# The first attention's heads between parts of the cross values' weight slots, with a third of the convolution's taps in its steps

## The chip, the cores and the metric

The kernel runs on one core of one Trainium2 chip. The metric is the device time of one execution in microseconds (us). Before the change three runs took 1483.89, 1485.74 and 1492.4 us, so the median is 1485.74 us.

## What is computed

Two blocks in a row over 256 tokens of width 1024, all in float32. Only the first block's mixer and the key and value projections of its cross attention matter here:

```python
y = rmsnorm(h, norm_mix_g[l]) @ w_in[l]
q = partial_rotary(y[..., 0:D_ATT].reshape(B, S, ATT_HEADS, HEAD_DIM))
k = partial_rotary(y[..., D_ATT:2 * D_ATT].reshape(B, S, ATT_HEADS, HEAD_DIM))
v = y[..., 2 * D_ATT:3 * D_ATT].reshape(B, S, ATT_HEADS, HEAD_DIM)
att = dilated_sliding_attention(q, k, v).reshape(B, S, D_ATT)      # 8 heads of 64
conv = conformer_conv(...)        # a * sigmoid(g), depthwise convolution of 31 taps, layernorm, silu
h = h + jnp.concatenate([att, conv], axis=-1) @ w_out[l]
xq = (rmsnorm(h, norm_x_g[l]) @ w_xq[l])
mn = rmsnorm(mem, norm_mem_g[l])
xk = (mn @ w_xk[l])               # cross keys, from the memory alone
xv = (mn @ w_xv[l])               # cross values, from the memory alone
```

After it come the cross attention, a multilayer perceptron and the second block's two layers, the last one with eight experts. None of that is touched.

## The kernel before, in words

Every engine's program is written out by hand in its own function (`pe` for TensorE, `act` for ScalarE, `dve` for VectorE, `pool` for GpSimd, `sp` for SyncE), and engines meet at semaphores: `mark` counts an event, `after(...)` gives the count to wait for. Each engine carries out its own program strictly in the written order.

**Weights** come in slots of 1 MB. A ring of three raw slots (`weights`) is filled by SyncE. ScalarE's `high(n)` (line 1395) writes the rounded high part of a slot in two halves, and VectorE's `low(n)` (line 1869) writes what is left, in two halves too; the pair is `weights_split`, which has room for two slots. So `high` of slot j waits until TensorE has used slot j-2, and each half of `low` waits for the same half of `high`. TensorE takes three matmuls per product (`matmul3`, lines 532 to 534): high by high, high by low, low by high. A slot costs it 48 matmuls of 256 columns (`features_out`) or 24 of 512 columns, 12 for each of the two token tiles (`tokens_out`). Slots 10 to 13 are the cross keys (`xk`), 14 to 17 the cross values (`xv`), 18 to 21 the output projection (`wout`).

**Order on TensorE** before the change: slots of `g`, `a`, `q`, `k`, then the memory's turned rows, `v`, four slots of `xk`, four slots of `xv`, then 16 transposes of queries and keys (line 704, `qkT`), and then `attention`. Results go to a ring of four banks (`open_bank`); a bank is reused once ScalarE or VectorE has read it.

**The attention** is pipelined over steps s. In step s TensorE does `scores` of head s (line 713, two matmuls from 64 rows), the four transposes of head s-1's probabilities (line 646) and `outs` of head s-2 (line 666, into 64 columns). ScalarE does the two exponentials of head s (line 1452) and copies head s-1's turned probabilities (line 1467). VectorE first divides head s-1's probabilities by their sums (lines 1983 and 1987), then reads head s's scores and takes the negated maximum (lines 2001 and 2009), and in odd steps from 5 on splits a finished pair of heads (lines 1874 and 1876). All three functions have a hook `between(s)` that is called at the end of each step; the first attention leaves it empty.

**The convolution** is VectorE's: `conv_taps(n)` does n taps of a pair of channel tiles (line 2050, two instructions each), 62 taps in all, spread between the slots' `low`. After the attention comes the convolution's mean over channels: TensorE's `cmean` (line 723) waits for the last tap, VectorE subtracts it (line 2102), ScalarE squares, TensorE sums again (`cvar`), and after the scaling, the silu and a split TensorE can use the convolution's half of the features. Meanwhile TensorE does the attention's half of the output projection.

Of the kernel before, what the change touches and what calls it, by code (L numbers as in the profile page):

```python
# [11 lines left out]
P = 128  # L12
S = 256
TT = S // P
# [123 lines left out]
def program(nc, A, out, points, stop):  # L138
    ctx = ExitStack()
    with ctx:  # L140
# [231 lines left out]
        def after(*name):  # L372

            key, n = points.get(name, ("pe", 1))
            return sems[key], n
# [139 lines left out]
        with nc.Block() as block:  # L515
# [3 lines left out]
            def _(pe):  # L519
# [25 lines left out]
                def tokens_out(stage, actT, n, i=0, tag=(), midway=lambda: None):  # L545

                    ps = []
                    for r in range(2):
                        if r == 1:
                            midway()  # L550
                        j, w = weights(stage)
                        for t in range(TT):
                            if r == 0:
                                ps.append(open_bank(stage, *tag, i, t))
                            for k in range(4):
                                mm = matmul3(ps[t][:, 0:n], lambda z: actT[:, z, 4 * r + k, t * P:(t + 1) * P],
                                             lambda z: w[:, z, k, :], r == 0 and k == 0, r == 1 and k == 3)
                            if r == 1:
                                mm.then_inc(*cpe.mark("filled", stage, *tag, i, t))
                            elif t == 1:  # L560
                                mm.then_inc(*cpe.mark("slot", j))
                    cpe.also("slot", j)
# [93 lines left out]
                def pair_outs(stage, tag, v, until_now=False):  # L656

                    def outs(h, pt, u):
                        if h % 2 == 0:
                            ps = open_bank(stage, *tag, h // 2)  # L660
                        else:
                            ps = bank_of[(stage, *tag, h // 2)]
                        o = 64 * (h % 2)
                        for kt in range(TT):
                            first = kt * P if until_now else 0
                            mm = pe.matmul(ps[o:o + HD, first:S], v[:, kt, h * HD:(h + 1) * HD],  # L666
                                           flat(pt)[:, kt * S:(kt + 1) * S - first],
                                           start=(kt == 0), stop=(kt == TT - 1))
                        mm.then_inc(*cpe.mark("o", u))
                        if h % 2:  # L670
                            cpe.also("filled", stage, *tag, h // 2)
                    return outs
# [19 lines left out]
                turn_norm(1)  # L692
                tokens_out("v", HT, 512)
                pe.wait_ge(*after("ht", 1))
                for i in range(4):
                    features_out("xk", MT, "xk", i)
                for i in range(2):
                    tokens_out("xv", MT, 512, i)
                pe.wait_ge(*after("rotated"))
                for b in range(4):  # L700
                    ps = open_bank("qkT", b)
                    for c in range(2):
                        for t in range(TT):
                            mm = pe.transpose(ps[:, c * S + t * P:c * S + (t + 1) * P],
                                              QK[:, t, (2 * b + c) * P:(2 * b + c + 1) * P], ident)
                    mm.then_inc(*cpe.mark("filled", "qkT", b))
                pe.wait_ge(*after("read", "qkT", 3))
                pe.wait_ge(*after("read", "v", 0, 1))

                def scores1(h, ps):  # L710
                    o = 64 * (h % 2)
# [2 lines left out]
                                       QKT[o:o + HD, 4 + h // 2, :], start=True, stop=True)  # L714
                    return mm

                attention(0, AH, scores1, pair_outs("att_o", (), V))

                def mean_over_channels(name, need, src):
                    pe.wait_ge(*after(need))  # L720
# [631 lines left out]
            def _(act):  # L1352
# [142 lines left out]
                high(2)  # L1495
                for t in range(TT):
                    copy_out(V[:, t, :], psum("v", 0, t)[:, :], "v", 0, t)
                for i in range(4):
                    high(1)
                    copy_out(XKT[:, 2 * i:2 * i + 2, :], two(psum("xk", i)), "xk", i)  # L1500
                for i in range(2):
                    high(2)
                    for t in range(TT):
                        copy_out(XV[:, t, i * 512:(i + 1) * 512], psum("xv", i, t)[:, :], "xv", i, t)
                act.wait_ge(*after("heads_selected"))
                for b in range(4):
                    copy_out(QKT[:, 2 * b:2 * b + 2, :], two(psum("qkT", b)), "qkT", b)
                attention(0, AH)

                act.wait_ge(*after("read", "cmean"))  # L1510
                do(act.activation(SIG[:, :, :], C[:, :, :], ACT.Square), "csq")
# [334 lines left out]
            def _(dve):  # L1846
# [218 lines left out]
                for i in range(4):  # L2065
                    if i == 2:
                        rows_norm(1, MEM)
                    conv_taps(4 if i < 2 else 2)
                    low(1)
                turned(1, "norm_mem_g", 0, MT, T1)  # L2070
                for _ in range(2):
# [15 lines left out]
                own()  # L2087
                do(dve.tensor_tensor(x1, r[0], r[1], ALU.subtract))
                do(dve.tensor_tensor(x2, r[2], r[3], ALU.add), "rotated")
                for i in range(8):  # L2090
                    low(1)
                    conv_taps(5 if i < 6 else 4)
                assert taps_done == [TAPS, TAPS]

                def outs1(h):
                    if h % 2:
# [21 lines left out]
                    dve.wait_ge(*after("csilu"))  # L2118
                    split(lambda z: CAT[:, z, 4:8, :], C[:, :, :], "convT")

                attention(0, AH, 0.125, flat(logc), outs1)
                conv_mean()
                conv_variance()
                conv_scaled()
# [599 lines left out]
```

## Time and profile before

| | before |
|---|---|
| median of three runs | 1485.74 us |
| the profiled execution's own time | 1483.83 us |
| its span | 1482.0 us |
| TensorE busy with matmuls | 94% of the span |
| VectorE busy | 74% |
| ScalarE busy | 56% |
| mean granted TensorE clock | 0.975 |

The span is what the profiler records of the profiled execution; that execution took 1.83 us more by the clock that times runs. Busy TensorE is not TensorE at its peak, because matmuls overlap. The granted clock is 1.00 at 2.4 GHz and 0.50 at 1.2 GHz.

### The profile page before, as it was taken

To read this page: it belongs to the slowest core of one execution; us is meant where nothing else is said; L and a number is where in the kernel's file an instruction comes from. 1 tells how busy PE (TensorE), PEld (TensorE's weight loads), DVE (VectorE), ACT (ScalarE), POOL (GpSimd) and SP (SyncE) were. 2 spreads that over 40 slices of the span, in tenths; PEclk is the share of its full clock that TensorE was granted. 3 is DMA by queue.
4 is the path that set the end of the run, shared out by engine and by line. 5 is a ranking of instruction groups with operands and counts; after the bars stand their busy time and mean duration, and the time that the engine had idled before them with its cause. 6 is when DMAs were issued, how large, how long until landed. Compare 5 with 4: busy or idle time off the path is not lost.

```text
span 1482.0 us, 21894 instructions
## 1 busy us (share of the span) xinstructions
PE 1400.0 (94%) x8173; PEld 1222.9 (83%) x8173; DVE 1089.7 (74%) x1582; ACT 830.9 (56%) x1145; POOL 56.1 (4%) x60
## 2 busy tenths in 40 slices
PE   4997999999999999999999998988999999999997
PEld 4885587989988987899999997767888888888886
DVE  3889565656557876655555888767898898898986
ACT  3444354543435754453434484435787787787784
POOL 0000000000002130000000013010000000000000
PEclk9998899999999999999999999997999999999998
DMA  7555042555654520455555450117998988988983
GB/s 272 173 169 170 0 143 86 171 192 179 198 182 133 170 73 1 141 169 175 197 177 193 130 171 29 58 43 284 369 334 308 376 313 312 372 322 298 378 320 120
DMA packets 162964, 292.76 MB, mean 198 GB/s; under 512 B 6832, under 2 KB 78924, under 8 KB 162764
## 3 DMA queue, kind: packets, MB, share of 16 engines
q1 hardware_dynamic: 162336, 291.08, 56.8%
q8 instruction: 50, 0.82, 0.2%
q10 hardware_dynamic: 556, 0.67, 0.1%
q14 instruction: 22, 0.18, 0.0%
HBM read 290.69 MB, written 1.05 MB: 197 GB/s over the span
## 4 chain that ended last, share of the span: by engine, by line
PE 82%; DVE 14%; ACT 2%; issue 1%; ACTq 0%; POOL 0%; DVEq 0%; POOLq 0%
PE bank L532 23%; PE bank L534 22%; PE bank L533 22%; DVE weights_split L1869 4%; DVE arena L2050 3%; PE bank L1169 2%; PE bank L990 1%; PE bank L981 1%; PE bank L1242 1%; PE bank L996 1%; PE bank L666 1%; PE bank L646 1%; PE bank L1008 1%; PE bank L1219 1%; DVE arena L2389 1%
## 5 line engine op out<-in xcount | busy, mean ns | idle before, releaser
L1869 DVE TENSOR_TENSOR weights_split<-weights,weights_split 128x1024 fp32r<-128x1024 f32 (+4 forms) x266 | 304.3, 1187 | 179.0 <-ACT weights_split L1395 178.9
L1395 ACT ACTIVATE weights_split<-weights 128x1024 fp32r<-128x1024 f32 (+4 forms) x266 | 258.5, 1022 | 282.1 <-PE bank L534 281.4
L532 PE MATMUL bank<-features_split,weights_split 128*128 128x256 f32 x912 | 262.7, 288 | 13.7 <-DVE weights_split L1869 4.7
L533 PE MATMUL bank<-features_split,weights_split 128*128 128x256 f32 x912 | 260.2, 285 | 0.0
L534 PE MATMUL bank<-features_split,weights_split 128*128 128x256 f32 x912 | 260.1, 285 | 0.0
L532 PE MATMUL bank<-weights_split,features_split 128*128 128x512 f32 (+3 forms) x560 | 217.1, 388 | 8.5 <-DVE features_split L1876 3.6
L534 PE MATMUL bank<-weights_split,features_split 128*128 128x512 f32 (+3 forms) x560 | 213.5, 381 | 0.0
L533 PE MATMUL bank<-weights_split,features_split 128*128 128x512 f32 (+3 forms) x560 | 213.4, 381 | 0.0
L532 PEld LDWEIGHTS bank<-features_split,weights_split 128*128 128x128 f32 x912 | 177.3, 194 | 17.4 <-DVE weights_split L1869 6.2
L533 PEld LDWEIGHTS bank<-features_split,weights_split 128*128 128x128 f32 x912 | 177.3, 194 | 0.5
L534 PEld LDWEIGHTS bank<-features_split,weights_split 128*128 128x128 f32 x912 | 177.2, 194 | 0.0
L532 PE MATMUL bank<-weights_split,hidden_split 128*128 128x512 f32 x376 | 148.4, 395 | 1.0 <-DVE weights_split L1869 1.0
L534 PE MATMUL bank<-weights_split,hidden_split 128*128 128x512 f32 x376 | 146.7, 390 | 0.0
L533 PE MATMUL bank<-weights_split,hidden_split 128*128 128x512 f32 x376 | 146.5, 390 | 0.0
L532 PEld LDWEIGHTS bank<-weights_split,features_split 128*128 128x128 f32 x560 | 106.3, 190 | 27.3 <-DVE features_split L1876 4.4
L534 PEld LDWEIGHTS bank<-weights_split,features_split 128*128 128x128 f32 x560 | 106.1, 190 | 17.9
L533 PEld LDWEIGHTS bank<-weights_split,features_split 128*128 128x128 f32 x560 | 106.3, 190 | 16.8
L2638 DVE TENSOR_TENSOR weights_split<-weights,weights_split 128x1024 fp32r<-128x1024 f32 x96 | 115.0, 1221 | 3.9 <-ACT weights_split L1734 2.8
L1734 ACT ACTIVATE weights_split<-weights 128x1024 fp32r<-128x1024 f32 x96 | 100.9, 1058 | 24.2 <-PE bank L534 24.0
L532 PEld LDWEIGHTS bank<-weights_split,hidden_split 128*128 128x128 f32 x376 | 70.7, 188 | 15.7 <-DVE weights_split L1869 2.0
L534 PEld LDWEIGHTS bank<-weights_split,hidden_split 128*128 128x128 f32 x376 | 70.6, 188 | 15.3
L533 PEld LDWEIGHTS bank<-weights_split,hidden_split 128*128 128x128 f32 x376 | 70.7, 188 | 13.7
(362 smaller groups left out, 2267.0 us busy)
## 6 DMA issues: line engine op xcount, KB each, us to landing
weights<-in_moe_gate_dram SPq DMA_DIRECT2D x26, 1024.0 KB, 6.6
weights<-in_moe_up_dram SPq DMA_DIRECT2D x24, 1024.0 KB, 6.7
weights<-in_moe_down_dram SPq DMA_DIRECT2D x24, 1024.0 KB, 7.3
weights<-in_w_in_dram SPq DMA_DIRECT2D x20, 1024.0 KB, 5.2
weights<-in_w_up_dram SPq DMA_DIRECT2D x16, 1024.0 KB, 5.2
weights<-in_w_down_dram SPq DMA_DIRECT2D x16, 1024.0 KB, 4.9
weights<-in_w_out_dram SPq DMA_DIRECT2D x12, 1024.0 KB, 5.0
weights<-in_ffn_gate_dram SPq DMA_DIRECT2D x11, 1024.0 KB, 5.3
```

Source lines behind the costliest of these rows:

```text
L532: pe.matmul(ps, lhs(0), rhs(0), start=start, stop=False, skip_group_check=shared)
L533: pe.matmul(ps, lhs(0), rhs(1), start=False, stop=False, skip_group_check=shared)
L534: return pe.matmul(ps, lhs(1), rhs(0), start=False, stop=stop, skip_group_check=shared)
L646: mm = pe.transpose(ps[:, at:at + P], pr[:, kt * P:(kt + 1) * P], ident)
L666: mm = pe.matmul(ps[o:o + HD, first:S], v[:, kt, h * HD:(h + 1) * HD], flat(pt)[:, kt * S:(kt + 1) * S - first], start=(kt == 0), stop=(kt ...
L981: mm = pe.matmul(inplace(ps[:, i * P:(i + 1) * P].unsqueeze(1), lev), LT[:, p, :], chosen(DI, p, 1, lev), start=True, stop=True)
L1169: mm = pe.matmul(ps[:, k * P:(k + 1) * P], XS[:, z, t, f * P:(f + 1) * P], GSEL[:, t, :], start=(t == 0), stop=(t == TT - 1))
L1395: do(act.activation(split_flat(j)[:, 0, part], raw_flat(j)[:, part], ACT.Copy), "hi", j, b)
L1734: do(act.activation(split_flat(j)[:, 0, part], raw_flat(j)[:, part], ACT.Copy), "hi_item", s, b)
L1869: do(dve.tensor_tensor(split_flat(j)[:, 1, part], raw_flat(j)[:, part], split_flat(j)[:, 0, part].bitcast(F32), ALU.subtract), "lo", j)
L2050: do(dve.scalar_tensor_tensor(C[:, i, :], U[:, i, k:k + S], w, C[:, i, :], ALU.mult, ALU.add), "conv")
L2638: do(dve.tensor_tensor(split_flat(j)[:, 1, part], raw_flat(j)[:, part], split_flat(j)[:, 0, part].bitcast(F32), ALU.subtract), "lo_item", ...
```

## The change

The cross values leave their place ahead of the attention. Their 96 matmuls stand in the attention's steps instead: step s of TensorE (s from 0 to 7) ends with half a slot, 12 matmuls of 512 columns (`cross_values`). The fourth slot of the cross keys moves behind the transposes of queries and keys. ScalarE has the `high` of slots 16 to 19 in steps 2, 4, 6 and 8, behind that step's exponentials and copy, and copies the values out in steps 3, 4, 7 and 8. VectorE has the `low` of slots 15 to 19 in steps 0, 2, 4, 6 and 8, each ahead of two taps, and two taps in every step from 0 to 9: 20 of the 62. Two taps fewer stand in the stretch of the q and k slots, and 20 instead of 38 between the rotation and the attention. The number of taps, matmuls and slots is the same.

```diff
@@ TensorE @@
-                for i in range(4):
+                for i in range(3):
                     features_out("xk", MT, "xk", i)
-                for i in range(2):
-                    tokens_out("xv", MT, 512, i)
                 pe.wait_ge(*after("rotated"))
...
+                features_out("xk", MT, "xk", 3)
                 pe.wait_ge(*after("read", "qkT", 3))
                 pe.wait_ge(*after("read", "v", 0, 1))
+                cross_slot = {}
+
+                def cross_values(s):
+                    if s >= 8:
+                        return
+                    i, r, t = s // 4, s // 2 % 2, s % 2
+                    if t == 0:
+                        cross_slot[i, r] = weights("xv")
+                    j, w = cross_slot[i, r]
+                    ps = open_bank("xv", i, t) if r == 0 else bank_of["xv", i, t]
+                    for k in range(4):
+                        mm = matmul3(ps[:, :], lambda z: MT[:, z, 4 * r + k, t * P:(t + 1) * P],
+                                     lambda z: w[:, z, k, :], r == 0 and k == 0, r == 1 and k == 3)
+                    if r == 1:
+                        mm.then_inc(*cpe.mark("filled", "xv", i, t))
+                        cpe.also("slot", j)
+                    elif t == 1:
+                        mm.then_inc(*cpe.mark("slot", j))
...
-                attention(0, AH, scores1, pair_outs("att_o", (), V))
+                attention(0, AH, scores1, pair_outs("att_o", (), V), between=cross_values)
@@ ScalarE @@
-                for i in range(4):
+                for i in range(3):
                     high(1)
                     copy_out(XKT[:, 2 * i:2 * i + 2, :], two(psum("xk", i)), "xk", i)
-                for i in range(2):
-                    high(2)
-                    for t in range(TT):
-                        copy_out(XV[:, t, i * 512:(i + 1) * 512], psum("xv", i, t)[:, :], "xv", i, t)
...
-                attention(0, AH)
+                copy_out(XKT[:, 6:8, :], two(psum("xk", 3)), "xk", 3)
+                high(1)
+
+                def cross_values(s):
+                    if s in (2, 4, 6, 8):
+                        high(1)
+                    if s in (3, 4, 7, 8):
+                        i, t = s // 4 - (s % 4 == 0), 1 - s % 2
+                        copy_out(XV[:, t, i * 512:(i + 1) * 512], psum("xv", i, t)[:, :], "xv", i, t)
+
+                attention(0, AH, cross_values)
@@ VectorE @@
-                    conv_taps(4 if i < 2 else 2)
+                    conv_taps(3 if i < 2 else 2)
...
-                for i in range(8):
-                    low(1)
-                    conv_taps(5 if i < 6 else 4)
-                assert taps_done == [TAPS, TAPS]
+                for i in range(4):
+                    if i < 3:
+                        low(1)
+                    conv_taps(5)
...
-                attention(0, AH, 0.125, flat(logc), outs1)
+                def beside_heads(s):
+                    if s in (0, 2, 4, 6, 8):
+                        low(1)
+                    if s < 10:
+                        conv_taps(2)
+
+                attention(0, AH, 0.125, flat(logc), outs1, between=beside_heads)
+                assert taps_done == [TAPS, TAPS]
```

Two places show how it moves instructions. The first is VectorE from the last slots ahead of the attention on. `weights_split<-weights,weights_split` is a `low`, `arena<-arena,vector_cols` are taps, `probs<-bank` is the read of the scores. Before, the steps hold nothing but attention:

```order
L1869 TENSOR_TENSOR weights_split<-weights,weights_split 128x1024 [waits scalar_done] x2
L2050 SCALAR_TENSOR_TENSOR arena<-arena,vector_cols 128x256 [waits vector_done] x8
L2001 SCALAR_TENSOR_TENSOR probs<-bank,shape_table 128x512 [waits matmul_done]
L2009 TENSOR_REDUCE negmax<-probs 128x2 [waits vector_done]
L1983 RECIPROCAL rden<-den 128x2 [waits scalar_done]
L1987 TENSOR_SCALAR probs<-probs,rden 128x256 [waits vector_done]
```

With the change, the same engine in steps 2 and 3:

```order
L2024 SCALAR_TENSOR_TENSOR probs<-bank,shape_table 128x512 [waits matmul_done]
L2032 TENSOR_REDUCE negmax<-probs 128x2 [waits vector_done]
L1892 TENSOR_TENSOR weights_split<-weights,weights_split 128x1024 [waits scalar_done] x2
L2073 SCALAR_TENSOR_TENSOR arena<-arena,vector_cols 128x256 [waits vector_done] x4
L2006 RECIPROCAL rden<-den 128x2 [waits scalar_done]
L2010 TENSOR_SCALAR probs<-probs,rden 128x256 [waits vector_done]
```

A `low`, which waits for ScalarE, and four tap instructions now stand between the negated maximum of head 2 and the division of its probabilities.

The second place is ScalarE in step 2. `probs,den<-probs,negmax` are the exponentials, `probsT<-bank` is the copy, `weights_split<-weights` is a `high`. With the change:

```order
L1469 ACTIVATE probs,den<-probs,negmax 128x256 [waits vector_done]
L1469 ACTIVATE probs,den<-probs,negmax 128x256
L1484 ACTIVATE probsT<-bank 128x512 [waits matmul_done]
L1412 ACTIVATE weights_split<-weights 128x1024 [waits matmul_done,weights_in1]
L1412 ACTIVATE weights_split<-weights 128x1024
```

Before, the four `high` of slots 16 to 19 stood ahead of the first exponential; now that of slot 16 stands behind head 2's exponentials, and those wait for VectorE.

## Rows read from the trace of the kernel before

**Rows 1.** The profile's page: granted clock in 40 slices, and the chain that ended last.
```profile
PEclk9998899999999999999999999997999999999998
...
PE 82%; DVE 14%; ACT 2%; issue 1%; ACTq 0%; POOL 0%; DVEq 0%; POOLq 0%
```
**Rows 2.** Timeline of DVE: start us, us, engine line op out<-in xcount [idle before <-releaser].
```profile
73.81 2.34 DVE L1869 TENSOR_TENSOR weights_split<-weights,weights_split 128x1024 fp32r<-128x1024 f32 x2
...
95.22 2.35 DVE L1869 TENSOR_TENSOR weights_split<-weights,weights_split 128x1024 fp32r<-128x1024 f32 x2
97.49 4.04 DVE L2050 SCALAR_TENSOR_TENSOR arena<-arena,vector_cols 128x256 f32<-128x256 f32 x10
101.45 2.36 DVE L1869 TENSOR_TENSOR weights_split<-weights,weights_split 128x1024 fp32r<-128x1024 f32 x2
...
143.48 0.70 DVE L2001 SCALAR_TENSOR_TENSOR probs<-bank,shape_table 128x512 f32<-128x512 f32 x1
...
146.06 0.17 DVE L1983 RECIPROCAL rden<-den 128x2 f32<-128x2 f32 x1 [1.16 <-ACT probs L1452]
146.26 0.62 DVE L1987 TENSOR_SCALAR probs<-probs,rden 128x256 f32<-128x256 f32 x2
...
172.55 0.43 DVE L1876 TENSOR_TENSOR features_split<-bank,features_split 128x256 fp32r<-128x256 f32 x1
...
178.59 1.22 DVE L2102 SCALAR_TENSOR_TENSOR arena<-bank,arena 128x1024 f32<-128x1024 f32 x1 [1.04 <-PE bank L723]
```
**Rows 3.** Timeline of PE around the first attention.
```profile
76.91 0.47 PE L532 MATMUL bank<-weights_split,features_split 128*128 128x512 f32 x1 [1.18 <-DVE arena L1887]
...
131.65 0.39 PE L532 MATMUL bank<-weights_split,hidden_split 128*128 128x512 f32 x1
...
134.14 0.40 PE L534 MATMUL bank<-weights_split,hidden_split 128*128 128x512 f32 x1
134.38 1.03 PE L704 MATMUL bank<-shape_table,arena 128*128 128x128 f32 x8
...
146.94 1.11 PE L646 MATMUL bank<-shape_table,probs 128*128 128x128 f32 x4 [5.24 <-DVE probs L1987]
...
163.01 1.13 PE L713 MATMUL bank<-arena 64*128 64x256 f32 x4
164.07 0.66 PE L646 MATMUL bank<-shape_table,probs 128*128 128x128 f32 x4
164.65 1.08 PE L666 MATMUL bank<-probsT,arena 128*64 128x256 f32 x4
...
176.56 1.99 PE L723 MATMUL bank<-arena,shape_table 128*128 128x256 f32 x8
...
193.35 0.60 PE L532 MATMUL bank<-weights_split,features_split 128*128 128x512 f32 x1 [2.11 <-DVE features_split L1876]
193.75 0.63 PE L533 MATMUL bank<-weights_split,features_split 128*128 128x512 f32 x1
```
**Rows 4.** Timeline of ACT.
```profile
72.03 2.00 ACT L1395 ACTIVATE weights_split<-weights 128x1024 fp32r<-128x1024 f32 x2 [3.43 <-PE bank L534]
...
144.94 0.51 ACT L1452 ACTIVATE probs<-probs,negmax 128x256 f32<-128x256 f32 x1 [4.08 <-DVE negmax L2009]
...
149.23 0.57 ACT L1467 ACTIVATE probsT<-bank 128x512 f32<-128x512 f32 x1
```
**Rows 5.** Windows: busy us of PE, PEld, DVE, ACT, POOL, then PEclk, DMA share, GB/s.
```profile
72.00:75.00 3.00, 1.15 (x11) 0.94 (x10) 3.00 (x7) 2.97 (x4) 0.00 (x0) 1.00 0.48 128
...
138.00:140.00 2.00, 0.71 (x5) 0.47 (x5) 2.00 (x3) 1.98 (x5) 0.00 (x0) 0.75 0.76 296
...
162.00:164.00 2.00, 2.00 (x7) 0.90 (x5) 0.78 (x3) 1.25 (x5) 0.00 (x0) 0.78 0.00 0
...
192.00:194.00 2.00, 0.65 (x2) 0.54 (x3) 1.97 (x3) 1.34 (x2) 0.00 (x0) 0.90 0.96 338
...
196.00:198.00 2.00, 2.00 (x8) 1.63 (x7) 0.00 (x1) 0.00 (x0) 0.00 (x0) 0.75 0.55 159
```

## The prediction

> **What bounds the kernel now.** I read the page first. TensorE holds 82% of the chain that ended last, and its granted clock is 9 or full in 38 of 40 slices, with the one 8 where the first attention lies [rows 1]. So outside this stretch the end is set by TensorE's own work, which the change leaves alone: what the change gains or loses must show as the time at which the stretch ends. I take as its end the start of the output projection's last part, at 193.35 us, where TensorE had stood idle for 2.11 us for the convolution's split [rows 3]. Then I read the timelines of the three engines around it. VectorE goes from a `low` at 95.22 without a gap to the attention at 143.48 [rows 2], while TensorE finishes the cross values at 134.4 [rows 3] and waits 5.24 us for the first probabilities. Inside the attention VectorE waits too, 1.16 us a head, for ScalarE's exponentials [rows 2]. So the idea has something to work with: TensorE and VectorE stand idle there in turn. Last the windows: the clock fell near 139.0, after some 4.5 us with little on TensorE but transposes, and was back only near 162.9; it fell again near 193.6, after the 2.11 us gap, and was back near 197.0 (each time from the share of a 2 us window) [rows 5]. At the lower level, 1.2 GHz, four transposes take 1.11 us against 0.66 at 2.4 GHz [rows 3].
>
> **Two taps fewer early.** The `low` at 73.81 begins when VectorE is free, though the first half of ScalarE's `high` ended near 73.0 (72.03 plus half of 2.00) [rows 2, 4]. 1.6 us less of taps lets it begin then, and TensorE's slot at 76.91 waits for what VectorE does next [rows 3]. Gain 0.7 us; everything up to the attention comes that much earlier.
>
> **VectorE up to the first head.** A `low` and five pairs of taps take 6.23 us (95.22 to 101.45) [rows 2]; a `low` is 2.27 of them, the ten tap instructions 3.96, so two pairs are 1.6. Three such rounds and one more of taps alone end at 94.5 + 18.7 + 4.0 = 117.2. TensorE is there before: `xk` 0 to 2 end at 104.5, the transposes with one wait for the copy of `xk` 2 at 107.6, the last `xk` slot at 113.4, the first scores and half a slot at 117.2. A VectorE step is 1.45 us for scores and maximum (143.48 to 144.94) and 0.73 for the probabilities (146.06 to 146.79) [rows 2, 4]. In step 0 come also a `low` and taps: 117.2 + 1.45 + 2.3 + 1.6 + 0.73 = 123.3 for the first probabilities, against 146.9 before. The transposes and half a slot (12 matmuls from 131.65 to 134.38, 2.7 us) and scores (1.06) put head 2's scores at 127.5 [rows 3].
>
> **The steps.** Here is the catch. In an even step VectorE reaches `low` right after the maximum, but ScalarE still has to do the exponentials (1.1 us), the copy (0.5) and the first half of the `high` (1.0) [rows 4]. So VectorE stands 2.6 us, with taps behind the `low` that could run. Then `low` 2.3, taps 1.6, probabilities 0.7; only then may TensorE turn them (0.6), do the outputs of the head before (1.0), half a slot (2.7) and the next scores (1.1) [rows 3], for which VectorE waits. The odd step between hides in this. Two steps thus take 1.45 + 2.6 + 2.3 + 1.6 + 0.7 + 0.6 + 1.0 + 2.7 + 1.1 = 14.1 us, 7.0 a head, against 3.3 for a head before (146.06 to 149.3) plus 5.4 of half a slot and scores. From 127.5: head 4's scores at 141.6, head 6's at 155.7, the probabilities of head 6 at 164.4, of head 7 at 169.0. Then the last transposes (169.7), copy and `high` (171.3), `low` and taps (175.2), a split of 0.87 (172.10 to 172.98, the second half in [rows 2]) and the last taps: 177.7. `cmean` takes 1.99 us and ends at 179.7; before it ended at 178.55 [rows 3]. With the clock always up the 22 us of cross values thus buy nothing: **+1 us**. What was 5 us of idle TensorE once is now a gap of 4.9 us ahead of the first transposes, one of 3.4 us in each of steps 3, 5 and 7, and one of 6 us ahead of `cmean`.
>
> **The clock.** The lower level before the change cost its share of the 178.55 already. With the change, TensorE does between two dense half slots around each of the 3.4 us gaps only scores, transposes and outputs: 6 us with 2.6 us of such work. That is about as thin as the stretch ahead of 139.0 (2.2 us of transposes in 4.6) and longer than the gap ahead of 193.6, after both of which the clock fell [rows 3, 5]. After 193.6 it was back in 3.4 us, since full matmuls followed. A spell of that length while TensorE is needed costs 1.7 us; one that lasts over transposes, outputs and half a slot (0.6 + 1.0 + 2.7 at double) costs up to 4. Four handoffs of probabilities come after a gap (heads 0, 2, 4, 6) and each lies on the path just added up. I take 2 us each, near the row of 197.0, the nearest: **+8**. The end of the attention leaves TensorE idle for 6 us, and `cmean` then runs at the lower level (1.65 us of issue to 3.3): **+1.7**.
>
> From 72 to 75 TensorE had only 1.15 us of work, nearly all of it transposes, and the clock stayed at 1.00 [rows 5]; going by that row transposes hold the clock and the sum stays as it is. The Trainium skill ("TensorE: Matmul & The Clock Gate", Part 4, on PE-mode transpose) says that transposes do not count as busy time for the clock; by that rule the spells last longer and the time is that of the third rival, 1504, and not of the sum.
>
> **Sum:** 1 + 8 + 1.7 = 10.7 us on the profiled execution's 1483.83 is 1494.5. The median of the runs lies 1.9 above that execution; I put the time at 1495. About 0.5%, 7.4 us, is what a measurement of this kernel can tell from no change. Bounds: no spell costs anything, +1; each of four costs 4 and the tail 2, +19.
>
> **The rivals.** *The spells fall mostly into the gaps themselves* and cost 0.5 to 1.5 us each: +3 to +7, 1487 to 1491. For it: the idle time of a gap is where a low clock is free. 14%. *The clock stays up,* as it did from 72 to 75 [rows 5]: +1, 1485 to 1487. For it: there are 96 full matmuls in these steps where there were none. 9%. *The clock, once down, stays down through the steps,* as from 139 to 162.9: a TensorE step is then near 10 us instead of 5.4 (transposes 1.1 [rows 3], scores and outputs about double their 1.1 and 1.0, and twelve matmuls of 0.40 us, 193.35 to 193.75, 4.8). Seven such steps from 123.3 on and a last half one end near 198 instead of 178: +20, 1504. Against it: full matmuls brought it back within 3.4 us at 197.0. 5%. *Faster:* VectorE doesn't wait for `high`, the one mechanism that lets its idle time be used. If ScalarE's halves were there in time in all four even steps, 2.6 us would go from each, the gaps would be below 1 us and the clock up: 177.7 minus 10.4, so about -9, 1475. It decides the sign as soon as more than one of the four waits is gone and the clock holds. Against it: the `high` stands behind exponentials that wait for that very step's maximum. 5%. *The change doesn't do what it says:* TensorE doesn't fill up because the first `low` in the steps comes late; that is the sum above with +1 and needs no case of its own.
>
> **How the numbers follow.** My case, +8 to +15, has 67%. Slower by over 0.5%: 67 + 5, 72%. Within 0.5%: 14 + 9, 23%. Faster: 5%. The range goes from 1486 (clock nearly always up) to 1503 (spells at their dear end), and leaves out the low end of the second rival, the 20 us case and the faster one.
>
> **What would show it.** VectorE's `low` in the steps should wait for ScalarE's `high`, four times, 2.2 to 2.7 us at full clock. The probabilities' handoffs should come every 14 to 17 us in pairs. TensorE should show gaps near 5, 3.4, 3.4, 3.4 and 6 us and the granted clock at 0.50 in or after most of them. `cmean` should end between 183 and 192 us, the last part of the projection start near 204 instead of 193.35, and every stage behind it should only be shifted. The prediction is wrong if the `low` finds its `high` ready, if the clock stays at 1.00 from 115 to 190, or if a later stage gives time back.

## The result and the profile after

The changed kernel takes 1494.46 us (median of 13 runs, 1493.98 to 1503.34) against 1485.77 us before (13 runs, 1478.79 to 1492.4). The ratio is 1.0073, with a 95% interval from 1.0057 to 1.0089: 0.73% slower.

| | before | after |
|---|---|---|
| profiled execution | 1483.83 us | 1496.93 us |
| span | 1482.0 us | 1495.1 us |
| last part of the output projection starts | 193.35 us | 205.71 us |
| mean granted clock | 0.975 | 0.971 |

The profiled execution after lies 2.5 us above its median, so its own 13.1 us more are somewhat too much; the ratio of the runs, 10.8 us on 1485.77, is the number to explain. The two medians alone differ by less, 8.7 us: the runs of the kernel before spread over 13.6 us, and the ratio weighs all of them.

The timeline of VectorE (start us, us, engine line op out<-in xcount, idle before and its releaser) shows the first head and one round of two heads, where [rows 2] had nothing but attention:

```profile
117.81 0.70 DVE L2024 SCALAR_TENSOR_TENSOR probs<-bank,shape_table 128x512 f32<-128x512 f32 x1
...
130.88 0.69 DVE L2024 SCALAR_TENSOR_TENSOR probs<-bank,shape_table 128x512 f32<-128x512 f32 x1 [3.44 <-PE bank L730]
...
134.89 2.36 DVE L1892 TENSOR_TENSOR weights_split<-weights,weights_split 128x1024 fp32r<-128x1024 f32 x2 [2.59 <-ACT weights_split L1412]
137.17 1.67 DVE L2073 SCALAR_TENSOR_TENSOR arena<-arena,vector_cols 128x256 f32<-128x256 f32 x4
...
146.86 0.69 DVE L2024 SCALAR_TENSOR_TENSOR probs<-bank,shape_table 128x512 f32<-128x512 f32 x1 [3.66 <-PE bank L730]
...
162.89 0.69 DVE L2024 SCALAR_TENSOR_TENSOR probs<-bank,shape_table 128x512 f32<-128x512 f32 x1 [2.94 <-PE bank L730]
...
180.80 2.36 DVE L1892 TENSOR_TENSOR weights_split<-weights,weights_split 128x1024 fp32r<-128x1024 f32 x2 [4.82 <-ACT weights_split L1412]
```

Heads 2, 4 and 6 are read at 130.88, 146.86 and 162.89, so 16 us go by for two heads. In each round VectorE waits twice, 2.59 us for ScalarE's `high` and 2.9 to 3.7 us for TensorE's scores. The chain of waits, followed back from the end through one such round, names each hand it passes through (start us, us, what):

```profile
130.88 0.70 DVE probs L2024
...
131.61 0.70 DVE negmax L2032
...
132.75 0.68 ACT probs L1469 x3
133.43 0.48 ACT probsT L1484
133.91 0.96 ACT weights_split L1412
...
134.89 2.36 DVE weights_split L1892 x2
137.25 1.58 DVE arena L2073 x4
...
139.62 1.12 PE bank L646 x4
140.73 1.90 PE bank L666 x4
142.63 0.59 PE bank L532
...
145.76 1.06 PE bank L730 x4
```

This is the loop of the forecast, link by link. The pieces left out are shorter: the division by the sums on VectorE, and the other eleven matmuls of the half slot. TensorE's timeline has the gaps, and the windows have the clock (columns as in [rows 5]):

```profile
123.87 1.11 PE L646 MATMUL bank<-shape_table,probs 128*128 128x128 f32 x4 [4.32 <-DVE probs L2010]
...
139.62 1.12 PE L646 MATMUL bank<-shape_table,probs 128*128 128x128 f32 x4 [3.16 <-DVE probs L2010]
140.66 1.97 PE L666 MATMUL bank<-probsT,arena 128*64 128x256 f32 x4
...
155.59 0.66 PE L646 MATMUL bank<-shape_table,probs 128*128 128x128 f32 x4 [3.15 <-DVE probs L2010]
156.18 1.59 PE L666 MATMUL bank<-probsT,arena 128*64 128x256 f32 x4
...
171.62 1.11 PE L646 MATMUL bank<-shape_table,probs 128*128 128x128 f32 x4 [3.17 <-DVE probs L2010]
...
187.17 3.73 PE L740 MATMUL bank<-arena,shape_table 128*128 128x256 f32 x8 [6.22 <-DVE arena L2073]
...
205.71 0.50 PE L532 MATMUL bank<-weights_split,features_split 128*128 128x512 f32 x1 [2.10 <-DVE features_split L1899]
```

```profile
122.00:124.00 2.00, 0.13 (x1) 0.14 (x2) 1.96 (x7) 0.00 (x0) 0.00 (x0) 0.62 0.49 121
...
128.00:130.00 2.00, 2.00 (x6) 1.35 (x6) 0.00 (x0) 0.00 (x0) 0.00 (x0) 0.68 0.00 0
...
136.00:138.00 2.00, 0.45 (x3) 0.05 (x1) 2.00 (x5) 0.00 (x0) 0.00 (x0) 1.00 0.00 0
138.00:140.00 2.00, 0.38 (x2) 0.39 (x3) 1.96 (x7) 0.00 (x0) 0.00 (x0) 0.88 0.83 161
140.00:142.00 2.00, 2.00 (x8) 1.08 (x6) 1.97 (x6) 1.08 (x5) 0.00 (x0) 0.50 0.95 368
142.00:144.00 2.00, 2.00 (x8) 1.22 (x7) 1.16 (x5) 0.97 (x3) 0.00 (x0) 0.76 0.00 0
...
154.00:156.00 2.00, 0.41 (x4) 0.41 (x4) 1.96 (x7) 0.00 (x0) 0.00 (x0) 1.00 0.79 184
156.00:158.00 2.00, 2.00 (x8) 0.86 (x7) 1.93 (x6) 1.11 (x5) 0.00 (x0) 0.65 0.88 340
...
184.00:186.00 2.00, 0.00 (x0) 0.00 (x0) 1.97 (x6) 0.00 (x0) 0.00 (x0) 0.50 0.73 238
```

The five gaps of 4.3, 3.2, 3.2, 3.2 and 6.2 us are each followed by work at the lower clock. After three of the four gaps ahead of transposes these take 1.11 or 1.12 instead of 0.66 us, and outputs 1.97 instead of 1.08. After the third gap, at 155.59, the transposes still take 0.66 us and only the outputs are slower, 1.59. `cmean` takes 3.73 instead of 1.99 [rows 3]. One detail shows why this is dear. From 136 to 138 TensorE has only 0.45 us of work and the clock is full; it falls near 139.5, as the work comes back, and is low until near 143.0. The third time it falls near 156.6, a microsecond after the work came back. Only ahead of `cmean` does a good part of a low spell lie in the gap: the clock is at 0.50 from 184 to 186, with TensorE idle until 187.17.

Behind 205.71 little changes. The kernel before had a low spell near 194 to 197 [rows 5] that the changed one has not, and of the 12.4 us there 10.75 are left at the start of the cross attention's output projection (250.83 and 261.58 us). The other 2.4 us of the 13.1 between the two profiled executions came in stages that the change doesn't touch.

### The profile page after: what moved, and what is told of

Read it like the earlier page. It is cut to its first block, busy times and chain, and to the rows that moved or that the text cites. A ratio compares the mean times of both kernels' runs of the same rounds, so it can differ in the third digit from the quotient of the medians.

```text
span 1495.1 us, 21894 instructions
## 1 busy us (share of the span) xinstructions
PE 1404.2 (94%) x8173; PEld 1227.2 (82%) x8173; DVE 1089.3 (73%) x1582; ACT 831.0 (56%) x1145; POOL 56.2 (4%) x60
## 4 chain that ended last, share of the span: by engine, by line
PE 83%; DVE 12%; ACT 3%; issue 1%; ACTq 0%; POOL 0%; DVEq 0%; POOLq 0%
PE bank L532 23%; PE bank L534 23%; PE bank L533 23%; DVE weights_split L1892 4%; PE bank L1186 2%; DVE arena L2073 2%; PE bank L1007 1%; PE bank L1259 1%; PE bank L998 1%; PE bank L1013 1%; PE bank L646 1%; PE bank L666 1%; ACT weights_split L1412 1%; PE bank L1025 1%; PE bank L1236 1%
## 5 line engine op out<-in xcount | busy, mean ns | idle before, releaser
L532 PE MATMUL bank<-weights_split,hidden_split 128*128 128x512 f32 x376 | 151.3, 402 | 0.0
L533 PE MATMUL bank<-weights_split,hidden_split 128*128 128x512 f32 x376 | 148.3, 394 | 0.0
L534 PE MATMUL bank<-weights_split,hidden_split 128*128 128x512 f32 x376 | 148.1, 394 | 0.0
L532 PEld LDWEIGHTS bank<-weights_split,hidden_split 128*128 128x128 f32 x376 | 72.0, 191 | 17.7 <-issue 1.5
L534 PEld LDWEIGHTS bank<-weights_split,hidden_split 128*128 128x128 f32 x376 | 71.7, 191 | 15.8
L533 PEld LDWEIGHTS bank<-weights_split,hidden_split 128*128 128x128 f32 x376 | 72.0, 191 | 13.9
```

The source lines that it names most:

```text
L532: pe.matmul(ps, lhs(0), rhs(0), start=start, stop=False, skip_group_check=shared)
L533: pe.matmul(ps, lhs(0), rhs(1), start=False, stop=False, skip_group_check=shared)
L534: return pe.matmul(ps, lhs(1), rhs(0), start=False, stop=stop, skip_group_check=shared)
```

## Experiments

The theory is that of the forecast: a loop of waits through three engines, which gives the cross values' room away, and on top the clock. Its rivals are that VectorE simply has too much to do in the steps (A), that ScalarE is late in any order (B), that the clock costs little (C), and that the taps alone do the harm (D). To compare landmarks between profiles I allow for the start: the last four transposes of `qkT` start at 107.89 us after the change and at 107.7 to 108.7 in its variants.

The variants ran in three sets, each beside new runs of the kernel before, whose medians were 1482.89, 1483.67 and 1483.64 us, not 1485.77. So variants are compared by their ratio to those runs, with its 95% interval in brackets. The ratio weighs all runs and differs from that of the medians by up to 0.0015, and a microsecond is 0.0007 of it.

**VectorE's taps ahead of its `low`.**

```diff
                 def beside_heads(s):
-                    if s in (0, 2, 4, 6, 8):
-                        low(1)
                     if s < 10:
                         conv_taps(2)
+                    if s in (0, 2, 4, 6, 8):
+                        low(1)
```

> The changed kernel, but VectorE's two pairs of taps stand ahead of the `low` in each step. Theory 1 (the changed kernel loses by a loop of waits of 14 us for two heads, in which VectorE waits 2.6 us for ScalarE's `high`, and by the lower clock that follows each gap of TensorE): the 1.6 us of taps go into the 2.6 us wait, so the loop is 1.6 us shorter, TensorE's gaps in steps 3, 5 and 7 shrink from 3.2 to about 1.6 us, the projection's last part starts near 196 instead of 205.7, and the time is about 1489 us, near before. Rival A (VectorE's own work in the steps sets the time: lows and taps are simply too much for it): its order changes nothing, 1494 to 1495 us.

Measured: 1487.99 us, ratio to before 1.0036 (1.0016 to 1.0056). The same instructions in another order, and half of the loss is gone by the ratios (1.0073 to 1.0036, intervals that just don't overlap). VectorE's timeline has the remaining wait, the rest of 2.6 less 1.6 us, and TensorE's the shorter gap:

```profile
148.70 2.36 DVE L1892 TENSOR_TENSOR weights_split<-weights,weights_split 128x1024 fp32r<-128x1024 f32 x2 [1.01 <-ACT weights_split L1412]
```

```profile
137.41 1.00 PE L646 MATMUL bank<-shape_table,probs 128*128 128x128 f32 x4 [1.58 <-DVE probs L2010]
...
151.84 0.65 PE L646 MATMUL bank<-shape_table,probs 128*128 128x128 f32 x4 [1.58 <-DVE probs L2010]
```

The projection's last part starts at 196.53 (forecast: near 196). A falls: VectorE's work was not the bound. After two of the three gaps of 1.58 us the clock still fell, so this gain too is partly one of the clock.

**ScalarE's `high` ahead of the exponentials.**

```diff
+                def high_ahead(s):
+                    if s in (2, 4, 6, 8):
+                        high(1)
+
                 def cross_values(s):
-                    if s in (2, 4, 6, 8):
-                        high(1)
...
-                attention(0, AH, cross_values)
+                attention(0, AH, cross_values, ahead=high_ahead)
```

> The changed kernel, but ScalarE does the `high` of steps 2, 4, 6 and 8 ahead of that step's exponentials. Theory 1: VectorE finds the high half ready, its four waits of 2.6, 2.6, 2.6 and 4.8 us go, the loop of two heads takes 11.5 us at full clock, TensorE's gaps in steps 3, 5 and 7 fall under 1 us and the clock stays up there; the projection's last part starts near 189 instead of 205.7, and the time is about 1482 us, 4 below before. Rival A (VectorE's own work): no change, 1494 us. Rival B (ScalarE is the one that is late, whatever its order): the exponentials come 2 us later instead, 1494 us or more.

Measured: 1479.27 us, ratio 0.9991 (0.9975 to 1.0006): not told apart from before, and 12 us better than the change as it stands. The waits for `high` in steps 2, 4 and 6 are gone (in step 8 VectorE still waits 1.46 us), two heads take 11.8 us, TensorE's gaps in steps 3, 5 and 7 are 0.48 us and the clock stays at 1.00 from 130 to 165:

```profile
142.33 0.69 DVE L2026 SCALAR_TENSOR_TENSOR probs<-bank,shape_table 128x512 f32<-128x512 f32 x1 [2.15 <-PE bank L730]
154.08 0.69 DVE L2026 SCALAR_TENSOR_TENSOR probs<-bank,shape_table 128x512 f32<-128x512 f32 x1 [1.35 <-PE bank L730]
```

```profile
136.60 0.66 PE L646 MATMUL bank<-shape_table,probs 128*128 128x128 f32 x4 [0.48 <-DVE probs L2012]
```

```profile
130.00:165.00 35.00, 33.56 (x147) 22.23 (x145) 29.93 (x64) 16.63 (x40) 0.00 (x0) 1.00 0.27 91
```

The last part starts at 190.58 (forecast: near 189), 15.1 us earlier than in the changed kernel. B falls, and A with it. The first handoff and `cmean` still run at the lower clock, 3.51 us for `cmean`.

**TensorE kept busy.** In `attention` the wait for the probabilities moves behind the wait for the bank, and between the two stand matmuls that nobody reads:

```diff
+                def keep_busy(s, ps):
+                    for _ in range({1: 18, 3: 13, 5: 13, 7: 13}.get(s, 0)):
+                        pe.matmul(ps[:, :], MT[:, 0, 0, 0:P], MT[:, 0, 0:2, :].rearrange("p a b -> p (a b)"), start=True, stop=True)
```

and 22 more stand ahead of `cmean`. They don't delay the transposes: these start 0.06 us after the probabilities are ready, here as in the changed kernel.

> The changed kernel, but TensorE does matmuls of 128 by 512 whose results nobody reads while it waits: 18 ahead of the first head's transposes, 13 in steps 3, 5 and 7 and 22 ahead of the channel mean, each set shorter than the gap it stands in. Nothing of the computation is left out. Theory 1 puts 8 to 11 us of the changed kernel's loss on the clock: the granted clock stays at 1.00 from 115 to 195, the loop of two heads takes 14 us instead of 16, the projection's last part starts near 194.5, and the time is about 1485 us, within 2 us of before. Rival C (the clock costs little, the waits alone make the loss): 1492 to 1494 us, although the clock is up.

Measured: 1486.54 us, ratio 1.0036 (1.0021 to 1.0051). The granted clock is 1.00 over the whole stretch, against 0.83 in the changed kernel (the same window of both; the first row is the filled kernel's):

```profile
115.00:195.00 80.00, 78.09 (x335) 55.93 (x334) 57.61 (x115) 34.80 (x67) 0.00 (x0) 1.00 0.23 72
```

```profile
115.00:195.00 80.00, 59.98 (x218) 40.81 (x217) 50.80 (x107) 27.83 (x58) 0.00 (x0) 0.83 0.20 66
```

The heads 2, 4 and 6 are read at

```profile
128.74 0.69 DVE L2033 SCALAR_TENSOR_TENSOR probs<-bank,shape_table 128x512 f32<-128x512 f32 x1 [0.96 <-PE bank L732]
...
143.17 0.69 DVE L2033 SCALAR_TENSOR_TENSOR probs<-bank,shape_table 128x512 f32<-128x512 f32 x1 [2.13 <-PE bank L732]
...
157.60 0.69 DVE L2033 SCALAR_TENSOR_TENSOR probs<-bank,shape_table 128x512 f32<-128x512 f32 x1 [1.34 <-PE bank L732]
```

so two heads take 14.4 us with the clock up, and the wait of 2.59 us for `high` stays. The last part starts at 196.20. That is 9.5 us earlier than in the changed kernel, and 9.9 us with the 0.35 us by which this profile is behind at the start. So much of the landmark comes from the clock. By the ratios of the runs it is less, 5.5 us. The forecast of "within 2 us of before" was missed by 3 us, though the landmark (194.5 expected) was missed by 1.7 only. C falls: adding 79 unread matmuls makes the kernel faster, with intervals that don't overlap.

**Only the cross values in the steps**, all taps ahead of the attention:

```diff
-                for i in range(4):
+                for i in range(8):
                     if i < 3:
                         low(1)
-                    conv_taps(5)
+                    conv_taps(5 if i < 6 else 4)
...
                     if s in (0, 2, 4, 6, 8):
                         low(1)
-                    if s < 10:
-                        conv_taps(2)
```

> The changed kernel, but with all of the convolution's taps ahead of the attention as before (only the cross values and their lows stand in the steps). Theory 1: VectorE gets to the first head at 132 instead of 117.8 us and TensorE waits 17 us for it; each pair of heads then takes about 12.5 us, the projection's last part starts near 204, the time is about 1493 to 1497 us. Rival D (the taps in the steps are what costs; the values alone belong there): clearly below 1490 us.

Measured: 1496.56 us, ratio 1.0098 (1.0077 to 1.0119), within the forecast of 1493 to 1497. It is the highest ratio of all, but its interval overlaps that of the change itself (1.0057 to 1.0089). TensorE waits for the first probabilities until 136:

```profile
136.37 1.12 PE L646 MATMUL bank<-shape_table,probs 128*128 128x128 f32 x4 [16.96 <-DVE probs L2010]
```

D falls: without the taps in the steps the kernel is not faster, since VectorE then comes late to the first head. That the taps in the steps help is not clear of the noise. The last part starts at 205.67, as in the changed kernel (205.71).

**Both orders.** The two edits above together.

> Both new orders in the changed kernel: ScalarE's `high` ahead of the exponentials, VectorE's taps ahead of the `low`. Theory 1: with the high half already there, the order of taps and lows matters only after the last head, where the `low` of slot 19 stands ahead of fewer taps; 0 to 1.5 us better than the high ahead alone, which had a ratio of 0.9991 to before: about 1478 us, ratio 0.998. Rival (the taps ahead save another 1.6 us for each pair of heads, as they did alone): ratio 0.995.

Measured: 1481.66 us, ratio 0.9997 (0.9982 to 1.0013), not told apart from the high ahead alone (0.9991), and above the rival's 0.995. The last part starts at 189.81. TensorE's gaps in the steps are 0.48 us in both. So the two edits work on the same wait: the high ahead removes it, and the order of the taps then adds nothing that these runs can tell. The taps ahead alone remove only 1.6 of its 2.6 us.

**The high ahead, and TensorE kept busy** (18 unread matmuls ahead of the first transposes, one in steps 3, 5 and 7, 11 ahead of `cmean`).

> The `high` ahead of the exponentials, and unread matmuls in what is left of TensorE's gaps: 18 ahead of the first head's transposes, one in steps 3, 5 and 7, 11 ahead of the channel mean. Nothing of the computation is left out. Theory 1: the clock stays up from 115 to 185, the projection's last part starts near 185.5, and the time is 2 to 4 us below the high ahead alone: ratio 0.996 to 0.998, about 1477 us. Rival C (the clock is worth little once the gaps are short): ratio 0.999 as without them.

Measured: 1480.04 us, ratio 0.9976 (0.9963 to 0.9989): faster than before by a quarter of a per cent. The last part starts at 186.93, with a start 0.8 us earlier than with the high ahead alone, so 2.9 us of the landmark are gained. In the times that gain is not clear: the interval overlaps that of the high ahead alone (0.9975 to 1.0006), so the rival of this run, that the clock is worth little once the gaps are short, is not excluded by them.

**The kernel before, kept busy:** 20 unread matmuls in the 5.24 us gap of [rows 3], 3 in the next step.

> The kernel before, with 20 unread matmuls in the 5.2 us gap ahead of the first head's transposes and 3 in the next step. Theory 1 (the kernel before paid for the lower clock from 139 to 163 as well, where TensorE's scores, transposes and outputs took 5 us a head against VectorE's 3.3): the clock is back near 146 to 150, the third, fourth and fifth head come at VectorE's 3.3 us, the attention ends 3 to 4 us earlier; ratio 0.997 to 0.998. Rival C: the clock costs the kernel before nothing, ratio 1.000 or, with the added work, above.

Measured: 1481.64 us, ratio 0.9986 (0.9969 to 1.0003), which is told neither from no change nor from the 0.997 to 0.998 expected. In the profile the mechanism is there: from the second head on each comes 3.3 to 3.4 us after the last, and `cmean` starts at 173.12 with a start 0.7 us later, so 4.1 us earlier than at 176.56 [rows 3]:

```profile
157.61 0.63 PE L648 MATMUL bank<-shape_table,probs 128*128 128x128 f32 x4 [0.60 <-DVE probs L1996]
...
160.91 0.63 PE L648 MATMUL bank<-shape_table,probs 128*128 128x128 f32 x4 [0.60 <-DVE probs L1996]
...
173.12 1.99 PE L729 MATMUL bank<-arena,shape_table 128*128 128x256 f32 x8
...
189.92 0.50 PE L532 MATMUL bank<-weights_split,features_split 128*128 128x512 f32 x1 [2.10 <-DVE features_split L1885]
```

This run matters for how the loss is shared out. The kernel before paid for the clock too, 4.1 us. With TensorE kept busy in both kernels the last part starts at 189.2 before (189.92 less 0.7) and at 195.85 after (196.20 less 0.35). So 6.6 us of the landmark's 12.4 are the longer loop, and the clock adds the other 5.8, the difference between 9.9 us after and 4.1 before. By the ratios (1.0036 and 0.9986) the loop is worth 7.4 us of the 10.8.

**The kernel before with only the taps moved.**

```diff
                 for i in range(8):
                     low(1)
-                    conv_taps(5 if i < 6 else 4)
+                    if i < 4:
+                        conv_taps(5)
...
-                attention(0, AH, 0.125, flat(logc), outs1)
+                def beside_heads(s):
+                    if s < 10:
+                        conv_taps(2)
+
+                attention(0, AH, 0.125, flat(logc), outs1, between=beside_heads)
```

> The kernel before, with only the taps moved: 20 taps in the attention's steps, the cross values ahead of the attention as before. Theory 1: VectorE gets to the attention earlier, but TensorE, whose cross values still stand ahead, lets the first head start no earlier than 140.7 instead of 143.5, and every step has 1.6 us more of VectorE's work of which 1.2 us fill its wait for the exponentials. 0 to 3 us slower than before, ratio 1.000 to 1.002. Rival D (taps in the steps are what costs): 1.004 or more.

Measured: 1485.04 us, ratio 1.0017 (1.0000 to 1.0034), as expected. The last part starts at 194.01, 0.7 us later than before, though VectorE was 0.6 us earlier at 94.59 us (95.22 in [rows 2]). Moving the taps alone costs 0 to 5 us. Moving the values alone costs 14.5 us and both together 10.8, two numbers that the intervals don't separate.

**Scores ahead of the half slot**, on top of the high ahead, with unread matmuls ahead of the first transposes and of `cmean` only:

```diff
                 def cross_values(s):
+                    if s + 1 < AH:
+                        if s >= 1:
+                            pe.wait_ge(*after("scores_read", s - 1))
+                        scores1(s + 1, SC_BANK[(s + 1) % 2]).then_inc(*cpe.mark("scores", s + 1))
```

> As the high ahead with unread matmuls (e6), but TensorE does the next head's scores ahead of a step's half slot of cross values instead of behind it; no unread matmuls in steps 3, 5 and 7. Theory 1 (the loop of two heads is a chain through VectorE, ScalarE and TensorE, of which 2.7 us are the half slot ahead of the scores): VectorE no longer waits 1.9 us for scores in steps 2, 4 and 6, the loop goes from 11.7 to TensorE's own 11.1 us, the projection's last part starts near 185 instead of 186.9, ratio to before about 0.996. Rival E (TensorE's own work is the bound once the high is ahead): no change, 0.9976 as in e6.

Measured: 1479.56 us, ratio 0.9961 (0.9942 to 0.9981). The interval overlaps that of the kernel without this edit (0.9976), and the profile shows no gain: the last part starts at 187.49 (forecast: near 185), with a start 0.7 us later than there. The gain that theory 1 promised failed to come, but its rival E, that TensorE is the bound, is not shown by it either, since TensorE still waits 0.56 us in steps 3, 5 and 7. The wait only moved. VectorE no longer waits for scores; it waits for `high` again,

```profile
142.11 2.36 DVE L1909 TENSOR_TENSOR weights_split<-weights,weights_split 128x1024 fp32r<-128x1024 f32 x2 [2.05 <-ACT weights_split L1427]
153.77 2.36 DVE L1909 TENSOR_TENSOR weights_split<-weights,weights_split 128x1024 fp32r<-128x1024 f32 x2 [1.26 <-ACT weights_split L1427]
```

because `high` of a slot waits until TensorE has ended the half slots of the one two before (ScalarE's `high` at 141.02 and 152.68 were idle 2.50 and 2.98 us for them), and these now come later than the scores. Two heads take 11.66 us (142.11 to 153.77), not the 11.1 expected.

**The first `low` a step later**, on top of that, with 6 unread matmuls ahead of the first transposes instead of 18.

```diff
-                    if s in (0, 2, 4, 6, 8):
+                    if s in (1, 2, 4, 6, 8):
                         low(1)
                     if s < 10:
-                        conv_taps(2)
+                        conv_taps((0, 2, 2, 3, 2, 2, 2, 2, 3, 2)[s])
```

> As e9, but VectorE's step 0 holds neither `low` nor taps; slot 15's `low` stands in step 1, and the two pairs of taps in steps 3 and 8. Six unread matmuls ahead of the first transposes instead of 18. Theory 1: the first probabilities come near 121 instead of 123.3 us, but VectorE's work between the first head and the last tap is the same 47 us and it now waits 1.1 us for the first exponentials: the projection's last part starts between 184 and 186, 0 to 1 us from e9, since VectorE's total work has become the bound. Rival E (TensorE is the bound): its gap of 4.3 us shrinks to 2, so 2 us better than e9.

Measured: 1479.55 us, ratio 0.9967 (0.9945 to 0.9989), no difference from the last. TensorE's first transposes start at 121.91 instead of 124.58, but the last part starts at 186.82 instead of 187.49: 2.7 us won at the first head shrink to 0.7 at the end. That is what theory 1 said of this step, not the 2 us of rival E, though the forecast of 184 to 186 was missed.

The last three kernels with the high ahead (0.9976, 0.9961, 0.9967) are faster than before by 0.2 to 0.4% and cannot be told from one another.

## Why the prediction was right

It said 1495 us; measured are 1494.46. The mechanism is the one that was forecast; that the number agrees within 0.6 us is in part luck. The sum of 10.7 us gives 1494.5 from the profiled execution, and 1496.4 from the median of the three runs then known, and 1495 was a choice between them. On the landmark the loss was 12.4 us, not 10.7, of which 1.6 were given back by 251 us. Step by step, against the trace:

- **What bounds the kernel.** In the main as put: the difference arises between 95 and 206 us. But later stages are not only shifted: of 12.4 us 10.75 are left at the cross attention's output projection, and the profiled executions end 13.1 apart. The forecast had named a later stage that gives time back as a sign of being wrong; 1.6 us of it is what happened. The reading of the clock was also too kind: the line in [rows 1] has a 9 in 36 of 40 slices, an 8 in three (two of them at the attention) and a 7 in one, far behind it.
- **Two taps fewer early, -0.7 us.** Wrong. The slot's `low` starts at 73.75, as at 73.81 in [rows 2]. Most of what the two taps freed was lost again in two waits that I had not followed back to: VectorE's next steps waited 0.50 us for ScalarE's `high` at 62.41 and 0.67 us for its sums of squares at 65.45. Nor does a gain there last: in the filled kernel that `low` starts at 72.48, 1.3 us earlier, and yet the first head is read 0.36 us later. So the first head is read at 117.81, not 117.2.
- **VectorE up to the first head.** Right but for that: probabilities at 123.8 against 123.3.
- **The steps.** The loop has the links that the sum gives, and the 2.6 us wait for `high` measured 2.59 us in three steps; the fourth, in step 8, took 4.82 us, and 2.38 in the filled kernel, so the rest of it was TensorE's lower clock. With the clock up, two heads take 14.4 us (forecast 14.1). Both orders that break the link, taps first and `high` first, move the landmark to within 0.5 and 1.6 us of where the loop puts it. The term "+1 us at full clock" is +2.5 in the filled kernel (196.20 - 0.35 - 193.35): 0.6 of the difference are the early taps, 0.7 the two rounds at 14.4. It is measured against a kernel before with its own low spell; with the clock up in both, the loop costs 6.6 us. The comparison with the step before has a slip that the sum doesn't use: half a slot and scores are 3.8 us, and 5.4 is TensorE's whole step.
- **The clock, +8 and +1.7.** The landmark gives 9.9 us for both, against 9.7. By the chain it is 2.5 at the first handoff, 1.6 at each of the next two, 2.4 at the last with the wait for `cmean`, and 1.8 at `cmean` itself (differences between the changed and the filled kernel's starts of heads 2, 4 and 6, of `cmean` and of the last part, each with the 0.35 us of the start added). "2 us each" was the right size, 8.1 us for the four.
- **Rival "the spells fall into the gaps".** Falls: near 139.5 the clock fell at the end of the gap, near 156.6 behind it, and of the spell from near 183.9 to 190.7 about half lay in the gap. **"The clock stays up"** falls for this kernel, and is what the filled one shows. **"Once down, stays down"** falls too: the clock was back after each spell, near 128.7, 143.0, 160.0 and 177.1, each time during half a slot of full matmuls. With it falls, for this kernel, the time of 1504 that the forecast tied to the rule of the Trainium skill ("TensorE: Matmul & The Clock Gate", Part 4, on transposes). Whether the rule itself holds for these transposes is not shown: no run here changes them alone. **"Faster"** needed `high` in time; the high ahead shows that this condition alone is worth 12 us, but even then the kernel can't be told from the one before. The rival's 9 us below it did not come: two heads then took 11.8 us, as 14.4 less 2.6 gives, but the first handoff and `cmean` kept their lower clock.

What stays open is the share of later stages. Against before, the changed kernel is 12.4 us later at the landmark and 10.8 slower by the ratio, but the filled one is 2.5 later and 5.3 slower, and the high ahead 3.6 earlier and only 1.3 faster. So 1.6 to 2.8 us arise behind the landmark, in either direction, and no run here shows where.

## What to carry to other kernels

Putting idle engines' work into another stage's steps was not free here, because it added links to that stage's loop: follow one item through all engines and write the loop's time before counting busy time. Where a step of one engine waits for another's that itself waits for the first one's result of the same step (here `low` behind `high` behind exponentials behind the maximum), issue the producer ahead of that first wait, which removed the wait here, or put independent work ahead of the waiting instruction, which removed as much of it as the work was long. And price TensorE's gaps twice, here even some of 1.6 us: once as idle time, and once as the half-speed work that follows them.

## What the runs showed of the hardware that I had not expected

- The clock fell after two of three gaps of only 1.58 us, next to which stood transposes and matmuls on 64 rows or into 64 columns (taps ahead of `low`; 0.89 in the window 136 to 138, 0.50 in 138 to 140). With the same work and gaps of 0.48 us (the high ahead) it stayed at 1.00 from 130 to 165.
- A fall can come at the end of a gap, so that the idle time is at full clock and the work behind it at half: 1.00 from 136 to 138 with 0.45 us of work on TensorE, 0.50 from 140 to 142 with TensorE busy throughout. It need not: it was 0.50 from 184 to 186 with TensorE idle. Nor did it come back only with full matmuls: in the kernel before it did so near 162.9 [rows 5], in the midst of transposes, scores and outputs.
- Unread matmuls in five gaps made the changed kernel faster by 0.4% (1.0073 to 1.0036 against before), although TensorE then does 79 matmuls more. With the smaller gaps of the high ahead, and in the kernel before, their gain was seen in the profile (2.9 and 4.1 us) and not clearly in the times.
